# Values product of full blocks in three fp32r passes, in 12 of 16 heads of a forgetting attention

## The reference

```python
logits = jnp.einsum('bhqd,bhkd->bhqk', q_blk, k).astype(jnp.float32) * scale
logits = logits + fq_blk[..., None] - fk[:, :, None, :]
logits = jnp.where(causal, logits, -jnp.inf)
p = jax.nn.softmax(logits, axis=-1).astype(v.dtype)
return jnp.einsum('bhqk,bkhd->bqhd', p, v)
```

## Time and profile before

| | us |
|---|---|
| median of 3 runs | 2956.42 (2955.02 to 2963.2) |
| profiled execution, its own time | 2945.81 |
| its span | 2944.3 |
| TensorE busy | 2898.1 (98%) |
| VectorE busy | 1797.9 (61%) |
| ScalarE busy | 1043.1 (35%) |
| mean granted TensorE clock | 0.996 of full |

### The profile page before, as it was taken

The page is one execution under the profiler, slowest core; times in us unless marked ns, Lnnn a source line. Parts: engine busy times, 40 slices in busy tenths (PEclk is TensorE's granted clock), DMA queues, the critical chain, the costliest instruction groups (busy, mean ns, idle before and its releaser), DMA issues.

```text
span 2944.3 us, 33309 instructions
## 1 busy us (share of the span) xinstructions
PE 2898.1 (98%) x12924; PEld 2338.6 (79%) x12924; DVE 1797.9 (61%) x2200; ACT 1043.1 (35%) x1340; POOL 339.6 (12%) x486
## 2 busy tenths in 40 slices
PE   7999999999999999999999999999999999999999
PEld 5788888777777888888888788876766888888887
DVE  6665556555547877676756344245454887768673
ACT  5111133323324333333335434334244433333331
POOL 1000000110002000111111001122121200011110
PEclk8999999999999999999999999999999999999999
DMA  6566546663222444564412324455352244475331
GB/s 237 182 210 239 202 156 221 224 232 116 61 89 86 157 158 157 204 225 166 149 31 104 123 72 140 144 135 118 87 118 80 97 172 157 147 262 181 136 136 58
DMA packets 186862, 439.49 MB, mean 149 GB/s; under 512 B 12977, under 2 KB 74852, under 8 KB 186724
## 3 DMA queue, kind: packets, MB, share of 16 engines
q0 software_dynamic: 61616, 222.34, 22.7%
q1 hardware_dynamic: 125108, 215.26, 22.0%
HBM read 314.09 MB, written 123.34 MB: 149 GB/s over the span
## 4 chain that ended last, share of the span: by engine, by line
PE 93%; DVE 3%; ACT 2%; DMA 1%; issue 1%; POOL 0%; ACTq 0%; DVEq 0%; POOLq 0%; SPq 0%
PE ps L2521 8%; PE ps L2522 8%; PE ps L2523 8%; PE ps L2687 6%; PE ps L2685 6%; PE ps L2689 6%; PE ps L2817 4%; PE ps L2359 4%; PE ps L2358 4%; PE ps L2355 4%; PE ps L2315 3%; PE ps L2318 3%; PE ps L2321 3%; PE ps L2447 3%; PE ps L2450 3%; PE ps L2451 3%
## 5 line engine op out<-in xcount | busy, mean ns | idle before, releaser
L2685 PE MATMUL ps<-z_hi,w_hi 128*128 128x512 f32 x768 | 298.8, 389 | 0.0
L2687 PE MATMUL ps<-z_lo,w_hi 128*128 128x512 f32 x768 | 298.8, 389 | 0.0
L2689 PE MATMUL ps<-z_hi,w_lo 128*128 128x512 f32 x768 | 298.8, 389 | 0.0
L2521 PE MATMUL ps<-h_hi,w_hi 128*128 128x512 f32 x576 | 224.4, 390 | 0.0
L2523 PE MATMUL ps<-h_hi,w_lo 128*128 128x512 f32 x576 | 224.1, 389 | 0.0
L2522 PE MATMUL ps<-h_lo,w_hi 128*128 128x512 f32 x576 | 224.1, 389 | 0.0
L2355 PE MATMUL ps<-z_hi,w_hi 128*128 128x512 f32 x512 | 203.4, 397 | 0.0
L2359 PE MATMUL ps<-z_hi,w_lo 128*128 128x512 f32 x512 | 199.4, 389 | 0.0
L2358 PE MATMUL ps<-z_lo,w_hi 128*128 128x512 f32 x512 | 199.3, 389 | 0.0
L1511 DVE TENSOR_TENSOR w_lo<-w_raw,w_hi 128x2048 fp32r<-128x2048 f32 x52 | 119.0, 2289 | 114.6 <-ACT w_hi L989 114.6
L1765 DVE SCALAR_TENSOR_TENSOR xT<-ps,ada,xT 128x512 f32<-128x512 f32 x128 | 93.9, 748 | 147.4 <-PE ps L2359 147.4
(11 more groups left out here) (379 smaller groups left out, 6650.9 us busy)
## 6 DMA issues: line engine op xcount, KB each, us to landing
t_s<-misc POOLq DMA_DIRECT2D x28, 1792.0 KB, 6.9
misc<-t_s POOLq DMA_DIRECT2D x98, 512.0 KB, 4.2
misc<-w_ada SPq DMA_DIRECT2D x80, 512.0 KB, 4.8
w_raw<-w_mlp_in SPq DMA_DIRECT2D x32, 1024.0 KB, 5.5
w_raw<-ret_w_in SPq DMA_DIRECT2D x24, 1024.0 KB, 8.1
x_s<-xT SPq DMA_DIRECT2D x12, 1024.0 KB, 6.6
xT<-x_s SPq DMA_DIRECT2D x12, 1024.0 KB, 11.1
a_bufs<-w_mlp_out SPq DMA_DIRECT2D x12, 1024.0 KB, 22.6
```

The lines of the kernel that those rows point to most:

```text
L2521: MM(out, hi, b_hi[:, k, :], start=k == 0 and i in (0, 1, 3), stop=False, skip_group_check=True)
L2685: MM(bank[at + m], hi, ring_b(z_hi, slot)[:, cols], start=first and i not in (2, 4, 5), stop=False, skip_group_check=True)
L2687: MM(bank[at + m], hi, ring_b(z_lo, slot)[:, cols], start=False, stop=False, skip_group_check=True)
L2689: mm = MM(bank[at + m], lo, ring_b(z_hi, slot)[:, cols], start=False, stop=last, skip_group_check=True)
```

## The change

In heads 2 to 7 and 10 to 15 the six full blocks of `values` become three fp32r matmuls each. For this ScalarE rounds the block to its high part (`p_high`, into slot 1 of `w_hi`), right behind its exponential. VectorE subtracts that from the block to get the rest (`p_low`, into slot 1 of `w_lo`). Both have two places in turn. The values of the next head are split the same way once per head (`v_split_high` behind block 8 on ScalarE, `v_split_low` behind `split_max` on VectorE); in heads 1 and 9 four fills of constants (`v_split_rest`) stand ahead of it. The third matmul of a block waits for the rest. The ring of probabilities has four places instead of eight in all heads, and pairs of semaphores are merged. VectorE's order is now the tuple `LOW_ORDER`: `z_low` stands behind the third row maximum instead of the fifth.

```diff
-        log_done, inv_done, y_read, y_gated = sem("log_done"), sem("inv_done"), sem("y_read"), sem("y_gated")
+        p_high_done, p_low_done = sem("p_high_done"), sem("p_low_done")
+        log_inv_done, y_read_gated = sem("log_inv_done"), sem("y_read_gated")
+        def y_read(count):
+            return 2 * count - 1
+        def y_gated(count):
+            return 2 * count
...
+        WIDE = [n for n, block in enumerate(fox_blocks) if block[3] == HALF]
+        v_high = sq_high[:].rearrange("p s (b n) -> p s b n", n=P)
+        v_low = [t[:, 1, S:2 * S].rearrange("p (b n) -> p b n", n=P) for t in (w_lo, w_hi)]
+        def is_split(h):
+            return h < FOX_HEADS and h % 8 >= 2
+        def ring_place(h, n):
+            return WIDE.index(n) % 2
+        def before_in_ring(h, n):
+            at = WIDE.index(n)
+            if at >= 2:
+                return h * NF + WIDE[at - 2] + 1
+            if h % 8 == 2:
+                return (h - 1) * NF
+            return (h - 1) * NF + WIDE[at + 4] + 1
+        V_SPLIT_AT = 8
+        LOW_ORDER = (0, "max1", "z", 4, "max3", 5, "max4", "y", 7, "max6", "split", "v", 9, "copy", 11)
...
-            return 4 + e % 4 if e < NF else e % 8
+            return 4 + e % 4
         def probs_before(e):
-            return e - 4 if e < NF + 4 else e - 8
+            return e - 4
...
+            def p_high(h, n):
+                e = h * NF + n
+                act.wait_ge(exp_done, e + 1)
+                act.wait_ge(pv_done, before_in_ring(h, n))
+                place = ring_place(h, n) * HALF
+                nc.scalar.activation(w_hi[:, 1, place:place + HALF], probs[:, probs_slot(e), :], ACT.Copy)\
+                    .then_inc(p_high_done, 1)
+            def v_split_high(h):
+                mine = slice(h % 2 * 64, h % 2 * 64 + 64)
+                act.wait_ge(fox_v_loaded[h % 2], 16 * (h // 2 + h % 2))
+                act.wait_ge(pv_done, (h - 1) * NF)
+                nc.scalar.activation(v_high[:, h % 2, :, mine], fv[:, h % 2, :, mine], ACT.Copy).then_inc(p_high_done, 1)
             for h in range(FOX_HEADS):
                 for n in range(NF):
                     exps(h, n)
+                    if is_split(h) and n in WIDE:
+                        p_high(h, n)
+                    if is_split(h + 1) and n == V_SPLIT_AT:
+                        v_split_high(h + 1)
...
+            def p_low(h, n):
+                place = ring_place(h, n) * HALF
+                hi, lo = (t[:, 1, place:place + HALF] for t in (w_hi, w_lo))
+                dve.wait_ge(p_high_done, p_high_count[h, n])
+                TT(lo, probs[:, probs_slot(h * NF + n), :], hi.bitcast(F32), ALU.subtract).then_inc(p_low_done, 1)
+            def v_split_low(h):
+                mine = slice(h % 2 * 64, h % 2 * 64 + 64)
+                dve.wait_ge(p_high_done, p_high_count[h, "v"])
+                TT(v_low[h % 2][:, :, mine], fv[:, h % 2, :, mine], v_high[:, h % 2, :, mine].bitcast(F32),
+                   ALU.subtract).then_inc(p_low_done, 1)
+            def v_split_rest(h):
+                dve.wait_ge(pv_done, h * NF)
+                for par in range(2):
+                    other = slice(64 - par * 64, 128 - par * 64)
+                    nc.vector.memset(v_high[:, par, :, other].bitcast(F32), 1.0).then_inc(p_low_done, 1)
+                    nc.vector.memset(v_low[par][:, :, other].bitcast(F32), 0.0).then_inc(p_low_done, 1)
             for h in range(FOX_HEADS):
-                if h % 8 == 0:
-                    next_max(h, (0, 1, 2, 3, 4, 5))
-                    y_gate(h, 0)
-                    next_max(h, (6, 7))
-                else:
-                    next_max(h, (0, 1))
-                    y_gate(h - 1, 1)
-                    next_max(h, (2, 3, 4))
-                    if h % 2 == 0:
+                for n in LOW_ORDER:
+                    if n in WIDE and is_split(h):
+                        p_low(h, n)
+                    elif n == "max1":
+                        next_max(h, (0, 1))
+                        if h % 8:
+                            y_gate(h - 1, 1)
+                        next_max(h, (2,))
+                    elif n == "z" and h % 2 == 0 and h % 8:
                         z_low(h // 2 - 1, 0)
                         z_low(h // 2 - 1, 1)
-                    next_max(h, (5,))
-                    y_gate(h, 0)
-                    next_max(h, (6, 7))
-                if h + 1 < FOX_HEADS:
-                    split_max(h + 1)
-                    copy_max(h + 1)
+                    elif n in ("max3", "max4"):
+                        next_max(h, {"max3": (3,), "max4": (4, 5)}[n])
+                    elif n == "y":
+                        y_gate(h, 0)
+                    elif n == "max6":
+                        next_max(h, (6, 7))
+                    elif n == "split" and h + 1 < FOX_HEADS:
+                        split_max(h + 1)
+                    elif n == "v" and is_split(h + 1):
+                        if h % 8 == 1:
+                            v_split_rest(h)
+                        v_split_low(h + 1)
+                    elif n == "copy" and h + 1 < FOX_HEADS:
+                        copy_max(h + 1)
...
-                keys = fv_first[:, b, :] if h == 0 else fv[:, h % 2, b, :]
-                MM(bank[6 + hf][:, HALF - w:HALF], keys, probs[:, probs_slot(e), 0:w],
-                   start=b == 0, stop=n in (HF0 - 1, NF - 1)).then_inc(pv_done, 1)
+                    pe.wait_ge(y_read_gated, y_read(v - 1))
+                out, last = bank[6 + hf][:, HALF - w:HALF], n in (HF0 - 1, NF - 1)
+                if is_split(h) and n in WIDE:
+                    place = ring_place(h, n) * HALF
+                    hi, lo = (t[:, 1, place:place + HALF] for t in (w_hi, w_lo))
+                    pe.wait_ge(p_high_done, p_high_count[h, n])
+                    if n == 0:
+                        pe.wait_ge(p_low_done, p_low_count[h, "v"])
+                    MM(out, v_high[:, h % 2, b, :], hi, start=b == 0, stop=False)
+                    MM(out, v_low[h % 2][:, b, :], hi, start=False, stop=False)
+                    pe.wait_ge(p_low_done, p_low_count[h, n])
+                    MM(out, v_high[:, h % 2, b, :], lo, start=False, stop=last).then_inc(pv_done, 1)
+                else:
+                    keys = fv_first[:, b, :] if h == 0 else fv[:, h % 2, b, :]
+                    MM(out, keys, probs[:, probs_slot(e), 0:w], start=b == 0, stop=last).then_inc(pv_done, 1)
```

More of the change, by code:

```diff
@@ L318, in build @@
         HF0 = 4
+        WIDE = [n for n, block in enumerate(fox_blocks) if block[3] == HALF]
[14 more added lines that the diff above has]
+        LOW_ORDER = (0, "max1", "z", 4, "max3", 5, "max4", "y", 7, "max6", "split", "v", 9, "copy", 11)
+        p_high_count, p_low_count = {}, {}
+        for h in range(FOX_HEADS):
+            for n in range(NF):
+                if is_split(h) and n in WIDE:
+                    p_high_count[h, n] = len(p_high_count) + 1
+                if is_split(h + 1) and n == V_SPLIT_AT:
+                    p_high_count[h + 1, "v"] = len(p_high_count) + 1
+        low_step = 0
+        for h in range(FOX_HEADS):
+            for n in LOW_ORDER:
+                if n == "v" and is_split(h + 1):
+                    if h % 8 == 1:
+                        low_step += 4
+                    low_step += 1
+                    p_low_count[h + 1, "v"] = low_step
+                elif is_split(h) and n in WIDE:
+                    low_step += 1
+                    p_low_count[h, n] = low_step
         def fox_tiles(h):
@@ L971, in _ @@
                 if h % 2 and h + 1 < FOX_HEADS:
-                    wait_run(y_gated, h * 2 + 2)
+                    wait_run(y_read_gated, y_gated(h * 2 + 2))
                     load_og(h // 2 + 1)
@@ L1462, in inverse_sum @@
                 if v >= 2:
[L1463 to L1466, removed]
+                    act.wait_ge(y_read_gated, y_read(v - 1))
+                nc.scalar.activation(log_sum[sums, n, :], bank[6 + n][sums, :], ACT.Ln).then_inc(log_inv_done, 1)
+                act.wait_ge(log_inv_done, 2 * v + 1)
+                nc.scalar.activation(log_sum[sums, n, :], log_sum[sums, n, :], ACT.Exp, scale=-1.0).then_inc(log_inv_done, 1)
             def z_high(pr, n):
                 cols = slice(HALF * n, HALF * (n + 1))
-                act.wait_ge(y_gated, pr * 4 + n + 3)
+                act.wait_ge(y_read_gated, y_gated(pr * 4 + n + 3))
                 nc.scalar.activation(z_hi[:, pr % 4, cols], y_fox[:, cols], ACT.Copy).then_inc(z_hi_done, 1)
+            def p_high(h, n):
[10 more added lines that the diff above has]
+                nc.scalar.activation(v_high[:, h % 2, :, mine], fv[:, h % 2, :, mine], ACT.Copy).then_inc(p_high_done, 1)
             for h in range(FOX_HEADS):
@@ L2227, in y_gate @@
                 v = h * 2 + n
-                dve.wait_ge(inv_done, v + 1)
+                dve.wait_ge(log_inv_done, 2 * v + 2)
                 if h % 2 == 0 and h:
```

(15 more changed lines are left out.)

1 line of the change is left out of this document (added).

## The result

The changed kernel takes 3017.47 us (median of 4 runs, 3010.81 to 3019.78) against 2956.73 us for the kernel before in the same comparison: ratio 1.0205, 95% interval 1.0188 to 1.0222, that is 61 us slower. The direction was forecast, the size wasn't: 2980 us, with a range to 2998.

The account below looks back on a forecast made before the run. TensorE was taken to bound the kernel, with VectorE level with it in even heads. Even heads 6 × 2.2, odd 5 × 1.0, landing 10 × 0.2, heads 1 and 9 2 × 1.4, head 15 1.0: 24.0 us onto 2956.4, 2980 us; range 2964 to 2998.

Parts of the forecast that it names:

- VectorE's run to the split: VectorE, second row maximum to split: three rests delay TensorE's transpose, 2.2 us per even head, 1.0 per odd.
- The tail gives nothing back: Head's end: block 11's exponential-rounding-rest chain eats 0.18 us saved on blocks 9 and 11; earlier savings precede a waiting transpose.
- The landing of the maxima: Split to next head's first logits: later copy lands among GpSimd's loads, 0.2 us in each of 10 heads (0 to 0.6).
- Heads 1 and 9: Between split and copy: four fills and one rest make the maxima land late, 1.4 us each.
- Head 15: No score tiles between blocks, so third passes lean on exponential, rounding and rest: + 1 us, between - 1 and + 3.
- Rival 3: Maxima land late, small packets queuing behind load packets 1 us or more in 10 heads: 2988 to 2995 us, chance 14%.
- Rival 1: VectorE keeps up and TensorE's saving stays, 0.72 us per head: 2946 to 2948 us, chance 7%.
- Rival 2: Gain and loss cancel: even heads lose say 1 us each, odd heads keep their saving: 2962 us, chance 7%.

Follow-up runs that it names:

- Loads behind the maxima: Changed kernel, with GpSimd's loads of head h + 3 held until the row maxima of head h + 1 have landed: 2982.89 us, 1.0096 to the kernel before.
- Without rests: Changed kernel without VectorE's subtraction p_low and the wait for it; third passes multiply what lies in the buffer: 2974.24 us, 1.0076 to the kernel before.
- the order alone: Changed kernel, no head split, first-half y_gate and z_low behind everything else on VectorE, ScalarE's inverse_sum one exponential later: 2953.48 us, 0.9996 to the kernel before.
- the split of five blocks in the new order: Changed kernel, block 11 unsplit, y_gate and z_low last on VectorE, copy before block 9's rest and fills, inverse_sum later: 2943.89 us, 0.9962 to the kernel before.

## Why the prediction was wrong in size

**VectorE's run to the split** (2.2 us in even heads, 1.0 in odd ones): right. Free of the collision and of falls of the clock ("Loads behind the maxima") the heads are 20.6 and 19.2 us against 20.3 and 19.0 forecast: 2.0 and 0.8 us more up to the transpose, 0.45 in both behind it. Three spare passes in the run of the kernel before lengthened its heads by 1.6 and 0.6 us.

**The tail gives nothing back**: right. Without rests 0.05 of 0.36 us was left, and block 11 costs where it stands last. That nothing comes back from blocks 0 to 7 was right too, but only in part for the reason given: without rests the larger part was lost to ScalarE's order at block 0, a wait that the prediction hadn't listed.

**"The landing of the maxima"**: the step that failed, at two places. I took the last small packet, at about 2026.0, for the landing. The trace of before has the landing itself, in the weight load of the next head's first logits, which waits for it:

```profile
2026.44 0.19 PEld L2796 LDWEIGHTS ps<-q,k 128*128 128x128 f32 x1 [0.26 <-DMA q<-low_tiles]
```

Undisturbed, the first logits can start 2.5 us behind the copy (2023.94), not 2.1; with the copy 1.4 us behind the split that alone is about the 0.2 to 0.4 us that I had. And I priced the company of GpSimd's loads at 0.2 us, at most 0.6, from how little they overlap. It is 1.3 to 2.5 us: the gaps above, less 2.5, sum to 13.4 us over eight heads. What the small packets do in head 10's end (2232 to 2233 us, DMA queues: packets, MB, share):

```profile
q0 software_dynamic: 80, 0.29, 95.6%
q1 hardware_dynamic: 16, 0.00, 1.8%
```

The last 16 small packets moved in that microsecond, among 80 of the loads. The last of them began at 2232.97, and the first logits started at 2234.24, 1.27 us behind it. Before, it was 0.42 us (2026.02, the last of the two in the earlier trace rows, and 2026.44). So 0.85 us of the 1.3 extra in this head lie behind the last packet, not in front of it; why the completion comes so late the traces don't show, and it stays open. That both kinds of DMA share the engines is also what the Trainium skill says (page "DMA: Bandwidth & Descriptors", Issuing engines are not separate DMA queues: they run on the same 16 engines and interleave, whichever engine issued them); the trace agrees, with queue 1's packets between those of queue 0.

**"Heads 1 and 9"**, 1.4 us each: the fills did delay the copy as worked out, to 2.9 us behind the split, but SyncE then issued behind GpSimd (1981.98 against 1980.99), and the gaps were 5.07 and 6.35 us. Measured 4.4 and 6.0 us; with the loads held it is 2.2.

**The clock** had no term at all. It fell in six heads (2, 3, 4, 7, 10, 13). By the table, with the gaps taken out: 24.71 - 1.57 - 20.56 = 2.6 us for head 2, 2.2 for head 13 against 19.2, 2.8 in the run with the loads held. Each of the six began behind a wait for the maxima, of 4.16, 1.58, 1.73, 2.50, 5.45 and 1.86 us. Four heads behind waits of 1.65, 1.58, 1.32 and 1.30 us (5, 6, 11, 12) kept the full clock, and so did one of the two behind 1.60 us with the loads held. So a wait makes the fall possible and not certain. What decides between the two stays open.

**Sum by the heads**, first logits of head 1 to those of head 15, against before: 24.6 us as with the loads held and without a fall (6 × 2.46 even, 4 × 1.22 odd, 0.65 for head 7, 2 × 2.16 for heads 1 and 9), 19.5 us for the collision (13.4 in the split heads, 6.1 in heads 1 and 9), 14.3 us for six falls of the clock: 58.4, as in the trace. Head 15 adds 1.5 (1.0 forecast). The profiled spans differ by 70.2 us; the other 10.3 lie ahead of head 1 (1964.60 against 1954.25), where nothing is split and where the profiled executions of all the runs vary between 1954 and 1968. For the first part the forecast had 23.0 us (24 with head 15). It came out as worked out but for heads 1 and 9, 4.3 us against 2.8. Rival 3 named the collision, at half its size, with a chance of 14%.

**Rival 1** (TensorE's saving stays) was out of reach for this order, even with free rests. **Rival 2** too: with the loads held and no fall of the clock even heads still lost 2.46 us, not 1, and odd ones lost 1.2.

## What to carry to other kernels

When an engine that looks idle on average is to take more work, follow its timeline back from the instruction that others wait for: the slack is what idles in that run, not the busy share. Before a small transfer on which the next stage waits is made later, look at what else will be in the queues then: here a copy 0.7 us later was the whole distance between 2.5 us and 4 to 5, and by the ratios one wait in the loads brought 32 us back and one reordered copy 39. A saving on the bounding engine showed here only once the streams of the others were reordered for it too: the order alone gave nothing, the split as first ordered cost 61 us, the split of five blocks in the new order gave 10.

## What the runs showed of the hardware

- A full 512-column product in three fp32r passes takes 0.68 us against 0.86 us as float32, about four fifths.
- The two small transfers issued from SyncE land 2.5 us behind the instruction that released them where GpSimd's first 256 KB load is issued 1.2 us behind SyncE (kernel before) or later. It was 3.8 to 5.0 us where that load is issued 0.4 to 0.6 us behind, and 5.1 to 6.4 us where it is issued 1 us ahead.
- A wait of 1.6 to 5.5 us on TensorE can be followed by a fall of its clock to 1.2 GHz, at a cost of 2.2 to 2.8 us; in four of seven cases that is more than the wait itself. Of nine waits of 1.3 to 1.9 us in two traces, five were not followed by one.
